# A projection stage whose weights are read during the stage before it, with a smaller tile in that earlier stage

## The reference

```
y = hybrid_mixer(x, ...)            # its last step: h @ w_out, h is (2048, 1280)
x = layer_norm(ALPHA * x + y, ln_g, ln_b)
h = layernorm(concat([meta, x]), ln_emb_g, ln_emb_b)          # 2064 rows
z = h @ w_in_2                                                # 1024 -> 1472
q_a, kv_a, k_pe, q_g, k_g, v_g = split(z)    # 256, 128, 64, 512, 256, 256
q  = rmsnorm(q_a) @ w_q_b;  kv = rmsnorm(kv_a) @ w_kv_b
q_m, k_m = q, kv with rotary positions on 64 of their columns
qg, kg = axial_rotation(rmsnorm(q_g)), axial_rotation(rmsnorm(k_g)); vg = v_g
return attention_and_experts(...)[:, 16:]    # the queries of the meta rows are not needed
```

## Time and profile before

| | us |
|---|---|
| median of 3 runs | 6454.59 |
| profiled execution, its own time | 6461.76 |
| its span | 6460.6 |
| TensorE busy | 5708.6 (88%) |
| VectorE busy | 3810.4 (59%) |
| ScalarE busy | 2269.0 (35%) |
| GpSimd busy | 755.1 (12%) |

### The profile page before, as it was taken

The page is one execution under the profiler, slowest core; times in us unless marked ns, Lnnn a source line. Parts: engine busy times, 40 slices in busy tenths (PEclk is TensorE's granted clock), DMA queues, the critical chain, the costliest instruction groups (busy, mean ns, idle before and its releaser), DMA issues. The chain is left out here.

```text
span 6460.6 us, 82625 instructions
## 1 busy us (share of the span) xinstructions
PE 5708.6 (88%) x26393; PEld 4516.7 (70%) x26394; DVE 3810.4 (59%) x7592; ACT 2269.0 (35%) x4436; POOL 755.1 (12%) x566
## 2 busy tenths in 40 slices
PE   8999896997999999979699998999988999888960
PEld 7777675775777777657577777777766777766750
DVE  6676584223555666657556465556566555666658
ACT  3444312333333344433233233334343232444421
POOL 1111053231000000025100000000000000000006
PEclk9999998998999999989799999999999999999985
DMA  3333333447111010042243444335455343565557
GB/s 132 114 114 108 122 114 108 136 125 221 57 46 40 20 42 22 9 139 82 98 175 141 163 152 164 146 144 187 173 205 205 120 157 130 201 225 212 199 188 257
DMA packets 278154, 871.47 MB, mean 135 GB/s; under 512 B 22305, under 2 KB 167313, under 8 KB 235665
## 3 DMA queue, kind: packets, MB, share of 16 engines
q1 hardware_dynamic: 228256, 744.21, 32.8%
q0 software_dynamic: 24576, 77.83, 3.6%
q10 hardware_dynamic: 24944, 45.37, 1.9%
HBM read 723.15 MB, written 144.18 MB: 134 GB/s over the span
## 5 line engine op out<-in xcount | busy, mean ns | idle before, releaser
L2401 DVE TENSOR_TENSOR e_wl<-r_raw,e_wh 128x1024 fp32r<-128x1024 f32 x772 | 908.4, 1221 | 405.1 <-DVEq L2203 397.8
L2310 PE MATMUL ps<-e_wh,e_hTh 128*128 128x512 f32 x2496 | 1026.8, 411 | 81.7 <-PEq L2203 81.7
L2310 PE MATMUL ps<-e_wl,e_hTh 128*128 128x512 f32 x2496 | 1002.0, 401 | 0.0
L2310 PE MATMUL ps<-e_wh,e_hTl 128*128 128x512 f32 x2496 | 1001.8, 401 | 0.0
L2352 ACT CAST e_wh<-r_raw 128x1024 fp32r<-128x1024 f32 x772 | 769.7, 1049 | 160.8 <-ACTq L2203 153.4
L2310 PEld LDWEIGHTS ps<-e_wh,e_hTh 128*128 128x128 f32 x2496 | 480.4, 192 | 203.7 <-issue 100.5
L2310 PE MATMUL ps<-e_wh,e_aTh 128*128 128x512 f32 x1248 | 519.7, 416 | 74.4 <-PEq L2203 74.4
L2310 PEld LDWEIGHTS ps<-e_wh,e_hTl 128*128 128x128 f32 x2496 | 478.7, 192 | 115.9
L2310 PEld LDWEIGHTS ps<-e_wl,e_hTh 128*128 128x128 f32 x2496 | 480.0, 192 | 103.9
L1614 PE MATMUL ps<-a_PT,a_V 128*128 128x512 f32 (+1 forms) x1088 | 548.9, 596 | 0.7 <-ACT a_oT L1670 0.7
L1683 DVE TENSOR_REDUCE a_sc<-ps 128x1 f32<-128x416 f32 (+1 forms) x640 | 365.1, 588 | 257.4 <-PE ps L1592 257.4
(11 more groups left out here) (357 smaller groups left out, 9613.6 us busy)
## 6 DMA issues: line engine op xcount, KB each, us to landing
r_raw<-in_wgu SPq DMA_DIRECT2D x130, 2048.0 KB, 8.4
r_raw<-in_wdn SPq DMA_DIRECT2D x64, 2048.0 KB, 8.0
m_raw<-in_w SPq DMA_DIRECT2D x56, 1024.0 KB, 4.9
yd<-e_Y ACTq DMA_DIRECT2D x156, 256.0 KB, 6.8
e_bg<-in_bgu SPq DMA_DIRECT2D x32, 1024.0 KB
qTd<-p_qt SPq DMA_DIRECT2D x32, 640.0 KB, 5.9
yd<-a_zt SPq DMA_DIRECT2D x32, 512.0 KB, 6.7
e_bd<-in_bdn SPq DMA_DIRECT2D x32, 512.0 KB, 8.9
```

What stands on the lines that cost most here:

```text
L2310: t = pe.matmul(E.G[g][:, :], x[:, b, k, :], y[:, c % 2, k, :], start=(n == 0), stop=(n == 23))
L2401: return dve.tensor_tensor(lo, src, hi.bitcast(F32), ALU.subtract)
```

## The change

1. The staging buffer `w2r` is held over both stages and now has all 8 rows of `w2`; SyncE loads them one by one in the join's iterations 3 to 10. In the projection stage some small buffers (`ra`, `rb`, `vt`, `sq`, `an`) are laid over it.
2. To make room, the join has 3 buffers for `wout` rows instead of 4, 2 for `h0` instead of 3, and its input is loaded and split per tile of 128 rows instead of per pair; `high(i + 1)` and `low(i + 1)` stand in iteration i.
3. In the projection, rows are transposed and split two tiles ahead (`turn(n + 2)`, between the second product and the small ones; two buffers for the halves). The banks are 4 for the products and 4 for the rest.
4. The first tile's product goes row by row of `w2` over its three banks, as the rows are split.
5. The meta rows are tile 8 instead of the last, without the parts that only queries need.

The core of the diff (`project_act`, `project_dve` and `project_pool` follow the same new order and leave out the query parts for the meta rows):

```diff
@@ join_stage
-    J.wor = sb("wor", [128, 4, 1024])
+    J.wor = sb("wor", [128, 3, 1024])
...
-    J.yr = sb("yr", [128, 2, 10, 256])
+    J.yr = sb("yr", [128, 2, 10, 128])
...
-    J.h0 = sb("h0", [128, 3, 1024])
+    J.h0 = sb("h0", [128, 2, 1024])
@@ join_sync
     rows(0)
+    rows(1)
     for k in range(10):
...
-    rows(1)
+    rows(2)
+    residual(0)
     sp.wait_ge(*J.g.at("add", -1, 1))
...
     for i in range(17):
         if i + 2 < 16:
             residual(i + 2)
-        if i < 16 and i % 2 == 0 and i // 2 + 2 < 8:
-            rows(i // 2 + 2)
+        if 1 <= i < 14:
+            rows(i + 2)
+        if 3 <= i < 11:
+            sp.dma_start(J.w2r[:, i - 3], A["w2"][:, i - 3, :]).then_inc(*J.w2ld.more())
@@ join_pe
     for i in range(2, 16):
         for n in range(2):
             p, f = opened(i, n)
-            if i % 2 == 0 and n == 0:
-                pe.wait_ge(*v.at("y", i // 2, 1))
+            if n == 0:
+                pe.wait_ge(*v.at("y", i, 1))
@@ join_dve
+    low(1)
...
         if i < 16:
             normal(i, 0, x, x)
-            if i % 2 == 0 and i // 2 + 1 < 8:
-                low(i // 2 + 1)
+            if 1 <= i < 15:
+                low(i + 1)
@@ project_stage
+TILES = list(range(8)) + [16] + list(range(8, 16))
...
-    P.hTh = sb("hTh", [128, 8, 128], F32R)
+    P.hTh = sb("hTh", [128, 2, 8, 128], F32R)
...
+    P.ra, P.rb = w2r[:, 0, 0:1024], w2r[:, 1, 0:1024]
...
-    P.bank = banks.turns(z, (0, 1, 2, 3, 4)) | banks.turns(b, (5, 6, 7))
+    P.bank = banks.turns(z, (0, 1, 2, 3)) | banks.turns(b, (4, 5, 6, 7))
...
+def squares(whole):
+
+    return range(8) if whole else (1, 6, 7)
+
+
+def wholes(n):
+
+    return sum(t < 16 for t in TILES[:n])
@@ project_sync
+    for n, t, r, whole in P.tiles:
+        if n >= 2:
+            sp.wait_ge(*P.g.at("yg", n - 2))
+            sp.wait_ge(*P.v.at("rot", n - 2))
+        sp.dma_start(P.rp[:, n % 2], A["rope"][t]).then_inc(*P.rpld[n % 2].more())
+        load(n + 2)
+        sp.wait_ge(*P.a.at("vn", n))
...
@@ project_pe
+    def row(n, m, k):
+
+        r, whole = P.tiles[n][2:]
+        lo, w = Z_COLS[m]
+        skip = 0 if whole or m else 256
+        p = ps[P.bank[("z", n, m)][0]]
+        for s, (x, y) in enumerate(((P.hTh, P.w2h), (P.hTh, P.w2l), (P.hTl, P.w2h))):
+            t = pe.matmul(p[0:r, skip:w], x[:, n % 2, k, 0:r], y[:, k, lo + skip:lo + w], start=(k == 0 and s == 0), stop=(k == 7 and s == 2))
+        return t
...
     turn(0)
+    turn(1)
+    pe.wait_ge(*v.at("x", 0, 1))
+    for k in range(8):
+        pe.wait_ge(*v.at("w2", k))
+        for m in range(3):
+            if k == 0:
+                opened("z", 0, m)
+            t = row(0, m, k)
...
     pe.wait_ge(P.const.sem, P.const.n)
-    for m in range(3):
-        project(0, m)
-    for i in range(NT):
-        n = rows_of(i)
-        if i + 1 < NT:
-            turn(i + 1)
-        project(i + 1, 0)
-        p, f = opened("an", i)
-        pe.wait_ge(*a.at("ak", i))
+    for n, _, r, whole in P.tiles:
+        project(n + 1, 0)
+        p, f = opened("an", n)
+        pe.wait_ge(*a.at("ak", n))
...
-        project(i + 1, 1)
-        p, f = opened("kn", i)
+        project(n + 1, 1)
+        turn(n + 2)
+        p, f = opened("kn", n)
@@ build
+    with nc.sbuf_tensor("w2r", [128, 8, 1472], F32) as w2r:
+        with ExitStack() as ctx:
+            J = join_stage(nc, A, banks, yTd, h0d, w2r, eps_ln, M, ctx)
...
```

More of the change, by code:

```diff
@@ L845, in join_stage @@
         now, back = i < 16, i >= 1
-        b = i // 2 + 1
-        ahead = now and i % 2 == 0 and b < 8
+        ahead = 1 <= i < 15
         a += [("sd", i, 0)] if now else []
-        a += [("y", b, q) for q in range(2)] if ahead else []
+        a += [("y", i + 1, q) for q in range(2)] if ahead else []
         a += [("sd", i - 1, 1)] if back else []
@@ L853, in join_stage @@
         v += [("rs", i, 0), ("ts", i, 0)] if now else []
-        v += [("y", b, q) for q in range(2)] if ahead else []
+        v += [("y", i + 1, q) for q in range(2)] if ahead else []
         v += [("rs", i - 1, 1), ("ts", i - 1, 1)] if back else []
@@ L868, in join_sync, with rows @@
     sp, A = nc.sync, J.A
[L870 to L873, removed]
+    def rows(i):
+        if i >= 2:
+            sp.wait_ge(*J.v.at("y", i - 2, 1))
+        lo = i % 2 * 128
+        sp.dma_start(J.yr[:, i % 2], J.yTd[i // 2, :, :, lo:lo + 128]).then_inc(*J.yld[i % 2].more())
     def residual(i):
@@ L1090, in project_stage @@
-    g = []
-    for i in range(NT):
[L1092 to L1099, removed]
-        g += [("gq", i), ("gk", i), ("sin", i), ("cos", i), ("yg", i)]
@@ L1101, in project_stage, with turned @@
-    P.bank = banks.turns(z, (0, 1, 2, 3, 4)) | banks.turns(b, (5, 6, 7))
+    P.tiles = [(n, t, rows_of(t), t < 16) for n, t in enumerate(TILES)]
+    z, b = [], [("x", n, hf) for n in range(2) for hf in range(2)]
+    a, v, g = [], [], []
+    def turned(what, n):
+        return [(what, n, 0), (what, n, 1)] if n < NT else []
+    for k in range(8):
+        a += [("w2", k)] + (turned("xh", 0) if k == 1 else []) + (turned("xh", 1) if k == 3 else [])
+        v += [("w2", k)] + (turned("x", 0) if k == 1 else []) + (turned("x", 1) if k == 3 else [])
@@ L1167, in turn, with project @@
             t.then_inc(f, 1)
-    def project(i, m):
-        if i >= NT:
+    def row(n, m, k):
[6 more added lines that the diff above has]
+        return t
+    def project(n, m):
+        if n >= NT or ("z", n, m) not in P.bank:
@@ L1171, in project @@
             return
-        n = rows_of(i)
-        lo, w = Z_COLS[m]
-        p, f = opened("z", i, m)
+        p, f = opened("z", n, m)
         if m == 0:
-            pe.wait_ge(*v.at("x", i, 1))
+            pe.wait_ge(*v.at("x", n, 1))
         for k in range(8):
-            if i == 0 and m == 0:
-                pe.wait_ge(*v.at("w2", k))
-            for s, (x, y) in enumerate(((P.hTh, P.w2h), (P.hTh, P.w2l), (P.hTl, P.w2h))):
-                t = pe.matmul(p[0:n, 0:w], x[:, k, 0:n], y[:, k, lo:lo + w], start=(k == 0 and s == 0), stop=(k == 7 and s == 2))
+            t = row(n, m, k)
@@ new lines, in project_pe @@
+    for k in range(8):
+        pe.wait_ge(*v.at("w2", k))
[3 more added lines that the diff above has]
+            t = row(0, m, k)
+            if k == 7:
+                t.then_inc(P.full[P.bank[("z", 0, m)][0]], 1)
+    pe.wait_ge(P.const.sem, P.const.n)
+    for n, _, r, whole in P.tiles:
+        project(n + 1, 0)
+        p, f = opened("an", n)
+        pe.wait_ge(*a.at("ak", n))
+        for k in range(0 if whole else 2, 3):
+            t = pe.transpose(p[:, k * 128:k * 128 + r], P.an[0:r, k * 128:(k + 1) * 128], ident[0:r, 0:r])
@@ L1246, in product, with turn @@
         return ps[P.bank[key][0]]
-    def turn(i):
-        n = rows_of(i)
+    def turn(n):
+        if n >= NT:
+            return
+        r = P.tiles[n][2]
         for hf in range(2):
-            p = product("x", i, hf)
-            if i and hf == 0:
-                act.wait_ge(*filled(P, ("z", i - 1, 2)))
-            act.copy(P.hTh[:, 4 * hf:4 * hf + 4, 0:n], p[:, :].rearrange("p (a b) -> p a b", a=4)[:, :, 0:n]).then_inc(*a.step("xh", i, hf))
+            p = product("x", n, hf)
+            if n >= 2 and hf == 0:
+                act.wait_ge(*filled(P, ("z", n - 2, 2)))
+            act.copy(P.hTh[:, n % 2, 4 * hf:4 * hf + 4, 0:r], p[:, :].rearrange("p (a b) -> p a b", a=4)[:, :, 0:r]).then_inc(*a.step("xh", n, hf))
```

499 lines of the change are left out of this document (248 added, 251 removed).

## The result

| | before | after |
|---|---|---|
| median of the runs | 6456.0 us (6452.6 to 6465.7) | 6663.25 us (6662.1 to 6668.6) |
| span of the profiled execution | 6460.6 | 6660.9 |
| TensorE busy | 5708.6 | 5750.0 |
| VectorE / ScalarE / GpSimd busy | 3810.4 / 2269.0 / 755.1 | 3803.8 / 2268.3 / 747.4 |

A forecast was written before the change was run, and what follows sets the result against it. The join was taken as bound by TensorE, which had no gap, so any wait there adds in full. Join +151 and projection +27.5 gave +178.5 us, on the median 6454.6 a forecast of 6633, range 6560 to 6670.

The forecast's parts named there:

- the two mechanisms: Join: TensorE waits for the split behind VectorE's chain, +151 us; projection: fourth bank waits for the rotation table, +50.4.
- one wait, tiles 3 to 15: Join: TensorE stands 9.8 us per tile: VectorE's chain 5.69, split 3.9 with GpSimd between its halves, signals 0.2.
- restart behind it: TensorE restarts at half clock after each wait and loses 1.5 us, bounds 0 and 2.4.
- tile 2's wait: Join: tile 2 comes behind two VectorE chains and waits 12.7 us instead of 9.73, +3.
- E_0 after the stage's first load: Projection: the first tile's last transposes end 49.9 us after the stage's first load instead of 71.8, -21.9.
- tile 7: Projection: its bank does not gate; VectorE's late turn to split rows two ahead does; 23 us, -3.1.
- tile 9: Projection: its rotation table stands behind small stores only; 27 us, +0.9.
- tail: Projection's end: last tile is now whole, so 30.7 us to the next stage's first load instead of 23.3, +7.4.
- The gate in the projection: Fourth bank is free only after VectorE's read, which needs the late rotation table: TensorE stands 5.7 us, period 30.3.
- b: Projection: the rotation table lands in time and does not gate the fourth bank; 6561 us, 12%.
- c: TensorE does not come back to full clock within a tile, +10.6 us for 13 tiles; 6771 us, 4%.
- d: Join: the split halves come in time, VectorE's chain off TensorE's path; the table still gates the projection; 6486 us, 5%.
- e: VectorE's chain gates neither stage; only the start, removed waits and shorter meta tile count, -40; 6415 us, 3%.

The follow-up runs named there:

- the best kernel: Changed kernel with join rows split at the iteration's head, rotation table issued ahead of the stores, meta rows last and five product banks: 6413.1 us, ratio 0.9929.
- both repairs: Changed kernel with the join's rows split at the head of the iteration and the rotation table issued ahead of the stores: 6427.3 us, ratio 0.9947.

## Why the prediction came out as it did

The sign, the two mechanisms and the order of their sizes were right. The 30 us between 6633 and 6663 are 22 by which the spans moved more than predicted (200.3 for 178.5), and 8 from the forecast standing on the median of the runs: the profiled execution before lay 7 us above its median, the one after 1 us below. The 22 are +10 in the join, -3.5 in the projection and +15 behind it. Step by step, with stages bounded by SyncE's first load, as in the prediction:

| term | predicted | measured |
|---|---|---|
| join, in all | +151 | +161.4 |
| one wait, tiles 3 to 15 | 9.8 | 9.57 |
| restart behind it | 1.5 | 2.6 and 1.6 in turn |
| tile 2's wait | 12.7 | 12.3 |
| start of the join | +1 | +3 |
| projection, in all | +27.5 | +24.0 |
| E_0 after the stage's first load | 49.9 | 45.7 |
| period of a whole tile | 30.3 | 30.5 |
| tile 7 | 23 | 25.5 |
| meta tile | 19.9 | 20.1 |
| tile 9 | 27 | 24.2 |
| tail | 30.7 | 29.5 |
| all behind the projection | 0 | +14.9 |

**The join.** Chain (5.69), split with GpSimd between its halves (3.70 for 3.9) and the wait were right, and so was the price of 31 us for GpSimd's multiplication (2.19 us in 14 tiles). The clock was priced too low. Half-clock products end after 5.56 and 3.46 us in alternate tiles, so a restart costs 2.1 on average, not 1.5. In all, from TensorE's start on tile 2 to its end on tile 15 it takes 155.5 us longer than before, 12.0 for each of the 13 waits in between where 11.3 were predicted: 9.57 of wait, 2.1 of restart, and 0.3 that the sum had no term for, half of it the last product before a wait, which ends 0.39 us after its start where the next would have started after 0.23. That is 8.5 of the 10 us that are missing. The other 2 are at the start, where ScalarE makes its first cast of `y` at 770.50 against 768.05 and TensorE's first product stands at 776.44 against 773.61.

Restarts after waits cost about 27 us in the join and 25 in the projection; the kernel before has some 12 of its own (seven of its projection tiles take 27 us where the others take 25.5, and tile 2 of the join starts slowly), so they make 40 us of the difference. The Trainium skill (TensorE: Matmul & The Clock Gate, Part 1: The HAM clock gate) puts the penalty of the ramp below 1% of a typical span and says not to fit a specific count of slow products. These 52 us are 0.8% of the span, so its figure is not contradicted by them, but the 40 are a fifth of what the change costs: without restarts the prediction would have been 67 below what was measured; with 1.5 it was 30 below.

**The projection's start** went better than predicted. TensorE turned the rows of two tiles in 3.35 us and the products behind them came at the full-clock spacing from the second on, 0.20 us for 448 columns, so the first tile's product was done at S + 22.8 and not S + 25.7, and the wait of 1.6 us predicted behind it did not come; E_0 came 4.2 us earlier. (The terms written down for E_0 add up to 50.05, not 49.9.)

**The gate in the projection** was right to a quarter of a microsecond in its end (product at E + 10.6, predicted 10.85), and a little wrong in how the wait is made up: 4.12 us and a 1.09 before it, because ScalarE's norm is waited for first; together 5.2 of the predicted 5.7. The scaled rows are there at E + 5.8, predicted 5.9. The restart is again 2.1 for 1.5, so the period comes out the same. The runs with five banks and with the early table show the cause, for their edits have nothing in common but this gate. One reading was not quite right: that the late table "costs nothing today". It cost 3.9 us at the end of the stage, as the run with the early table in the kernel before shows.

**Tile 7** has a wait that the text did not name. Its rows' load is late too:

```profile
1418.31 0.60 PE L1269 MATMUL ps<-ident,w2r 128*128 128x128 f32 x4
1424.87 0.88 PE L1227 MATMUL ps<-ident,w2r 128*128 128x128 f32 x3 [3.81 <-ACT w2r L1322]
1430.24 1.97 PE L1186 MATMUL ps<-ident,p_ht 128*128 128x128 f32 x8 [4.49 <-DMA p_ht<-h0d]
```

The rows of two tiles ahead are loaded behind the last tile's stores, as the table is. A whole tile has 24 products more between these and its transposes, and hides it; tile 7 has not. In the kernel with the table early the rows' load still stands behind the stores, and the wait is still there:

```profile
1396.48 1.97 PE L1192 MATMUL ps<-ident,p_ht 128*128 128x128 f32 x8 [4.30 <-DMA p_ht<-h0d]
```

With the meta rows last there is none. The step said that VectorE's late turn decides; it is the rows' load, and 2.5 us more. Tile 9, priced at 27, takes 24.2: it has, like the tiles of the kernel with the early table (24.6), no wait for the table, and this takes back the 2.5 and a little more. The projection's total is closer than its terms: -4.2 at the start, -2.8 in tile 9 and -1.2 in the tail stand against +2 in the whole tiles and +2.7 in tiles 7 and 8, which is luck.

**What was not foreseen** is the last line of the table: +14.9 us behind the projection, in stages whose code is the same. None of it is attention: the 4 us by which attention is longer from mark to mark (1248.2 against 1244.2) lie ahead of its first load and are counted in the projection's tail. The routing takes 3 us less, the part behind the experts 1.4 more, and the experts 16.8 more: 3148.0, 3148.9 and 3150.9 us in three traces of the kernel before and its variant, 3159.0 to 3172.7 in all eleven of the kernel after and its variants. Busy time by stretch over that stage, before:

```profile
3103.90:6251.90 3148.00, 2863.13 (x12480) 2281.92 (x12480) 1855.66 (x3917) 1133.86 (x1617) 122.34 (x112) 0.96 0.47 170
```

and after:

```profile
3286.10:6450.90 3164.80, 2874.76 (x12480) 2290.20 (x12480) 1854.41 (x3917) 1133.95 (x1617) 118.97 (x111) 0.96 0.46 170
```

TensorE's instructions are as many, it is busy 11.6 us more, and the clock is the same to two digits. Over all traces the busy time does not tell the two groups apart (2863 to 2869 us against 2864 to 2878); what does is the rest of the stage, in which TensorE is idle: 280 to 285 us in the three, 290 to 296 in the eleven. So about 10 us of idle time go with the change and survive every repair. It stands before the products of line 2310: TensorE waits there for 155 to 156 us in the three and for 161 to 168 in the eleven. These waits go through the helper that takes a semaphore (line 2203), so the profile doesn't name for whom. Without the longer experts' stage the gain of the best kernel would be some 20 us larger. It is none of the parts that the runs took out one at a time: the two orders, the fourth bank, the place of the meta rows, the first tile row by row, the loads ahead. All eleven kernels keep the rest: the rows split tile by tile, the buffer held over both stages, the transposes two tiles ahead, and later code that lies elsewhere in the program. Which of these it is, no run tells. Its cause stays open.

**The rivals.** The rotation table does gate (b, 6561); the clock comes back (c, 6771); the join does not split in time (d, 6486); and nothing ended on the other side (e, 6415). Three of their figures can be held against runs that made their conditions true; to each come the 15 us above and the 6 by which the kernel before was slower on that chip. With the split in time the kernel takes 6506.4, against 6486 for d, with the additions 6507. With the table early it takes 6588.85, against 6561 for b, with them 6582. With both repairs it takes 6427.3, against 6415 for e, with them 6436.

## What to carry to other kernels

An instruction that another engine needs next does not belong behind the wait for that engine's last result: in an order written by hand, look at what stands between two engines' turns, since the same split, moved ahead of one wait on each of its engines, was worth 157 us here. A buffer ring made one shorter, or one turn of its use moved, must be checked against the latest reader of the buffer, and this reader's own inputs: a load of 192 KB behind four stores cost 3.9 us at the end of the stage until the ring brought it onto the path of every tile, and 75 us then. And look at a change's parts separately: weights loaded ahead and the first product row by row were worth 13 and 9 us, each taken away alone, and were buried under two orders that cost 232.

## What was not expected of the hardware

Restarts of TensorE differ from tile to tile though the wait before them is the same 9.57 us: 13 products at half clock in one tile, 8 in the next, in turn, and periods of 26.0 and 25.0 us with them. Behind a wait of 4.12 us, 2.1 us were lost as well, hardly less than behind twice that. After 26 us of idleness the granted clock was back at 1.00 by the first product, behind nothing but 16 transposes (3.35 us). What makes the restarts differ is not shown.

The size of one effect was expected, and is worth keeping: two instructions of VectorE in a row, 0.78 us each, take 3.70 together when a multiplication of GpSimd starts between them, and 1.51 when it doesn't.
